# Delta rule of a two-model chain: gate rows in two buffers, strict matrices made two halves ahead, last merge on 64-wide blocks

## The chip, the cores and the metric

The kernel runs on 1 core of one Trainium2 chip. The metric is the device time of one execution in microseconds (us), 2837.27 us as the median of three runs. TensorE (PE), VectorE (DVE), ScalarE (ACT), GpSimd (POOL) and SyncE (SP) each work through a queue of their own in order; they meet only at semaphores. SP does nothing here but issue DMAs and wait.

## What is computed

The reference is a chain of layers on 528 tokens of width 1024, all in float32. The change touches one part of the first layer, the chunked gated delta rule over 16 value heads (`chunk_gated_delta_rule`):

```python
cum = jnp.cumsum(g, axis=-1)
decay = jnp.exp(jnp.where(causal, cum[..., :, None] - cum[..., None, :], -jnp.inf))
k_beta = k * beta[..., None]
a = jnp.where(strict, jnp.einsum('bhnid,bhnjd->bhnij', k_beta, k) * decay, 0.0)
sol = lax.linalg.triangular_solve(a + eye, rhs, left_side=True, lower=True, unit_diagonal=True)
u, w = sol[..., :dv], sol[..., dv:]
attn = jnp.einsum('bhnid,bhnjd->bhnij', q, k) * decay
def step(state, xs):
    v_new = u_c - jnp.einsum('bhck,bhkv->bhcv', w_c, state)
    o = jnp.einsum('bhck,bhkv->bhcv', q_c, state) + jnp.einsum('bhij,bhjv->bhiv', attn_c, v_new)
    state = state * last_c[..., None, None] + jnp.einsum('bhck,bhcv->bhkv', k_c, v_new)
```

Beside it the layer needs z, a projection of the same input (1024 to 2048 columns), whose blocks the kernel computes in the gaps of the delta rule.

## The kernel before

All of it is written out by hand, engine by engine, with semaphores; no planner chooses an order. The delta rule works on chunks of 106 tokens (`CH`), 5 of them, and on 8 of the 16 heads at a time: `HALVES` = 10 steps t, each two groups x of four heads. A step is called a half below. `pe_gdn`, `act_gdn`, `dve_gdn`, `pool_gdn` and `sp_gdn` hold one engine's part each, and in each a function `half(t)` or a loop over t.

A half needs the following, under the names of the profile.

- **Gate rows.** `g_D` (112 partitions x 8 heads x 106) is filled by a DMA that copies each head's cumulative gate to all partitions (`cum_rows`, L1214). `differences` subtracts the token's own gate (L1028) and adds a mask of large negative numbers (L1032), `decays` takes the exponential (L984), and `matrices` multiplies by beta (L1038) and by the product of keys that `kk` left in PSUM (L876, L1042). The result `g_AT` is the strict matrix of the half, in two buffers by t % 2. `decayed` makes `g_AN` = q k times decay (L1047) and is the last reader of `g_D`.
- **Small inverses.** `blocks_out` writes `g_AT` to HBM (L1222) and reads its 16x16 diagonal blocks back as `g_X`, one block to a partition (L1224). `small_inverses` (L1054 to L1086, blocks of 4, merged to 8) and `last_inverses` (to 16, then L1094 transposes) invert them on DVE. `blocks_back` (L1228, L1232) spreads them again as `g_blk`, and GpSimd's `expand` (L1173) makes block-diagonal matrices `g_U` and `g_TV` of them.
- **Merges.** Three times (`MERGES`, l = 0, 1, 2) the inverse grows by a level: TensorE transposes `g_U` (L927, not for l = 0), ACT copies that (L996), TensorE multiplies by `g_AT` (L938), ACT copies (L999), TensorE multiplies by `g_U` (L948), and DVE writes the new block under a mask (copy_predicated, L1135). All of it on the full 106x106.
- **State.** The value residual (L1107) reads the state `g_S`, which the half before wrote. After the merges TensorE applies the inverse (L955), DVE scales (L1141), TensorE makes the output and the state's increment (L965 to L969), GpSimd decays the state (L1188), DVE adds (L1145). Then L1047 makes `g_AN` of the next half.
- **z block.** In halves 0 to 5 TensorE also computes block z = t + 2 (`z_block`, 96 matmuls of L285 in two tiles), DVE evacuates each tile (`z_out`, L1101) into the one buffer `z_st`, and SP stores it (L1209). Its banks are those of the merges, so the merges wait for both. DVE splits weights for a later block at the half's end (L308), after which SP loads a new weight block (L2234). Halves 6 to 9 have no z block.

In half t, DVE's queue before is: keys (L1116), `differences(t+1)`, query decay (`g_EC`, L1123), `matrices(t+1)`, residual, both `z_out`, merge copy l = 0, `small_inverses(t+1)`, merge copy l = 1, `last_inverses(t+1)`, merge copy l = 2, L1141, then state and `g_AN` for each group, and the weight split. SP's queue, in half t, is `cum_rows(t+1)`, `blocks_out(t+1)`, two z stores, `blocks_back(t+1)`, `decay_rows(t+1)` (`g_EC`, L1217), the next weight load. `cum_rows(t+1)` waits until `g_AN` of half t is made, and `z_out` waits until the store before it has landed.

## Time and profile before

| | us |
|---|---|
| median of three runs | 2837.27 |
| lowest and highest | 2835.69, 2837.76 |
| profiled execution, its own time | 2833.87 |
| span of that execution | 2832.0 |
| ten halves of the delta rule in it | 309.6 to 714.7 |

The profile is one execution. Its page gives busy time of each engine, a chain of work that ended last, and groups of instructions by line. TensorE is busy for 91% of the whole span, but in 40 slices its digit falls to 7 or 8 in some of those that the delta rule covers, and the DMA engines move few bytes there. Times in the rows below count from the span's start.

### The profile page before, as it was taken

Reading aid. Unit: us, or ns where it says so; the run is one execution under the profiler, and the core shown is the slowest. Engines: PE = TensorE matmul, PEld = TensorE weight load, DVE = VectorE, ACT = ScalarE, POOL = GpSimd, SP = SyncE. Lnnn points to the kernel's source line nnn. Section 1 sums busy time; section 2 is a strip of 40 time slices with the busy share of each in tenths; the row PEclk is TensorE's granted clock in tenths of the full one; section 3 lists DMA queues with packets and bytes.
Section 4 is the critical chain, followed back from the end, with each engine's and each line's share of the span. In section 5 each row is a group of like instructions: output and inputs, shape, how many; then the busy total and the mean of one; then the engine's idle time right before and its main releaser. Section 6 shows DMA issues by size and latency. Waiting matters only on the chain.

```text
span 2832.0 us, 39867 instructions
## 1 busy us (share of the span) xinstructions
PE 2587.9 (91%) x16152; PEld 2269.9 (80%) x16152; DVE 1454.4 (51%) x2004; ACT 801.6 (28%) x1031; POOL 204.1 (7%) x166
## 2 busy tenths in 40 slices
PE   6998888868899999998998899999898778999998
PEld 6997888857799999998987688887685444688886
DVE  5776555655345344453364567667414555434433
ACT  5322222212422212231222322223222354323222
POOL 1000101011000000010000100002001200100001
PEclk9997999989699999999976999999898889899998
DMA  3222222231122222222200254444221000122221
GB/s 125 87 75 71 78 78 74 59 86 31 76 78 88 90 90 89 89 99 81 76 13 0 89 178 165 152 158 163 97 74 45 0 0 0 61 103 89 96 97 60
DMA packets 91921, 230.90 MB, mean 82 GB/s; under 512 B 59946, under 2 KB 61564, under 8 KB 67620
## 3 DMA queue, kind: packets, MB, share of 16 engines
q1 hardware_dynamic: 86272, 197.04, 21.6%
q10 hardware_dynamic: 5540, 32.30, 3.3%
q8 instruction: 82, 1.34, 0.2%
q14 instruction: 27, 0.22, 0.0%
HBM read 217.67 MB, written 11.64 MB: 81 GB/s over the span
## 4 chain that ended last, share of the span: by engine, by line
PE 78%; DVE 11%; DMA 4%; ACT 3%; issue 2%; POOL 0%; DVEq 0%; SPq 0%; ACTq 0%; POOLq 0%
PE ps L285 60%; DMA g_D<-scr_g 2%; PE ps L449 2%; PE ps L475 1%; PE ps L948 1%; PE ps L938 1%; PE ps L289 1%; DVE wlo L308 1%; PE ps L2122 1%; PE ps L2104 1%; DVE g_tmp L1082 1%; PE ps L1571 1%; PE ps L1572 1%; PE ps L955 1%; DVE a_mx L2188 1%
## 5 line engine op out<-in xcount | busy, mean ns | idle before, releaser
L285 PE MATMUL ps<-xa_hi,whi 128*128 128x264 f32 (+1 forms) x2512 | 656.4, 320 | 44.0 <-DVE wlo L308 19.8
L285 PE MATMUL ps<-xa_lo,whi 128*128 128x264 f32 (+1 forms) x2512 | 652.1, 319 | 0.0
L285 PE MATMUL ps<-xa_hi,wlo 128*128 128x264 f32 (+1 forms) x2512 | 649.8, 318 | 0.0
L308 DVE TENSOR_TENSOR wlo<-raw,whi 128x2048 fp32r<-128x2048 f32 x161 | 373.5, 2320 | 261.2 <-ACT whi L301 261.2
L285 PEld LDWEIGHTS ps<-xa_hi,whi 128*128 128x128 f32 x2512 | 419.2, 191 | 86.6 <-issue 33.2
L301 ACT ACTIVATE whi<-raw 128x2048 fp32r<-128x2048 f32 x161 | 307.5, 1910 | 598.0 <-PE ps L285 581.1
L285 PEld LDWEIGHTS ps<-xa_lo,whi 128*128 128x128 f32 x2512 | 419.4, 191 | 29.7
L285 PEld LDWEIGHTS ps<-xa_hi,wlo 128*128 128x128 f32 x2512 | 418.6, 191 | 30.3
L285 PE MATMUL ps<-xb_hi,whi 128*128 128x264 f32 (+1 forms) x1280 | 384.0, 340 | 9.9 <-DVE xb_lo L1688 8.1
L285 PE MATMUL ps<-xb_lo,whi 128*128 128x264 f32 (+1 forms) x1280 | 385.1, 341 | 0.0
L285 PE MATMUL ps<-xb_hi,wlo 128*128 128x264 f32 (+1 forms) x1280 | 383.6, 340 | 0.0
L285 PEld LDWEIGHTS ps<-xb_hi,whi 128*128 128x128 f32 x1280 | 220.5, 188 | 44.1 <-DVE xb_lo L1688 9.0
L285 PEld LDWEIGHTS ps<-xb_hi,wlo 128*128 128x128 f32 x1280 | 220.4, 189 | 27.5
L285 PEld LDWEIGHTS ps<-xb_lo,whi 128*128 128x128 f32 x1280 | 220.2, 189 | 27.6
L360 POOL TENSOR_TENSOR n_sq<-n_sq 128x512 f32<-128x512 f32 (+1 forms) x42 | 78.7, 1874 | 1403.1 <-ACT n_sq L370 1400.9
L643 DVE TENSOR_TENSOR h<-ps,h 128x528 f32<-128x528 f32 (+1 forms) x88 | 61.4, 698 | 189.1 <-PE ps L285 189.1
L580 ACT ACTIVATE xb_hi<-m_y 128x512 fp32r<-128x512 f32 (+1 forms) x96 | 61.1, 637 | 304.8 <-DVE m_y L620 280.7
L623 DVE TENSOR_TENSOR xb_lo<-m_y,xb_hi 128x512 fp32r<-128x512 f32 (+1 forms) x96 | 67.0, 698 | 67.5 <-ACT xb_hi L580 67.5
L645 DVE SCALAR_TENSOR_TENSOR h<-ps,b_mod,h 128x512 f32<-128x512 f32 x40 | 30.0, 751 | 123.2 <-PE ps L285 123.2
L938 PE MATMUL ps<-g_TV,g_AT 106*106 106x106 f32 x480 | 62.3, 293 | 30.4 <-DVE g_AT L1042 30.3
L938 PEld LDWEIGHTS ps<-g_TV,g_AT 106*106 106x106 f32 x480 | 58.6, 205 | 31.9 <-issue 30.8
L754 DVE SCALAR_TENSOR_TENSOR conv_acc<-conv_in,par,conv_acc 128x528 f32<-128x528 f32 x96 | 73.8, 769 | 11.3 <-DVE conv_acc L751 0.2
(386 smaller groups left out, 2919.8 us busy)
## 6 DMA issues: line engine op xcount, KB each, us to landing
raw<-weights SPq DMA_DIRECT2D x161, 1024.0 KB, 4.9
mod_w<-weights_mod ACTq DMA_DIRECT2D x24, 1024.0 KB, 4.8
g_EC<-scr_g SPq DMA_DIRECT2D x10, 424.0 KB, 4.8
scr_z<-z_st SPq DMA_DIRECT2D x16, 264.0 KB, 2.4
g_D<-scr_g SPq DMA_DIRECT2D x10, 371.0 KB, 6.2
scr_a<-g_AT SPq DMA_DIRECT2D x10, 318.0 KB
h<-x_in ACTq DMA_DIRECT2D x4, 528.0 KB, 8.2
z_a<-scr_z SPq DMA_DIRECT2D x1, 2112.0 KB, 12.4
```

What stands on the lines that cost most here:

```text
L285: mm = pe.matmul(ps[:, at_ + step * c + bank, 0:tn], w[:, hb.slot, k, c * P:(c + 1) * P], x[:, k, t0:t0 + tn], start=(k == 0 and n == 0), ...
L289: mm = pe.matmul(ps[:, 2 * c + 1, 0:en], w[:, hb.slot, k, c * P:(c + 1) * P], (elo if n == 1 else ehi)[:, k, 0:en], start=(k == 0 and n == ...
L301: act.activation(whi[:, hb.slot], raw[:, hb.raw_slot], ACT.Copy).then_inc(S("w_hi"), 1)
L308: dve.tensor_tensor(wlo[:, hb.slot], raw[:, hb.raw_slot], whi[:, hb.slot].bitcast(F32), ALU.subtract).then_inc(S("w_lo"), 1)
L360: pool.tensor_tensor(flat(sq[:, 0], pieces), flat(sq[:, 0], pieces), flat(sq[:, k], pieces), ALU.add)\
L449: mm = pe.matmul(ps[0:size, 4, bass.ds(i * (2 * heads) + (j * n * heads + first * heads), heads)], sq[:, buf, t:t + size], ones[:, 0:1] if ...
L580: act.activation(flat(xb_hi[:, t], pieces), flat(m_y[:, c], pieces), ACT.Copy).then_inc(S("two_hi"), 1)
L623: dve.tensor_tensor(flat(xb_lo[:, t], pieces), flat(m_y[:, c], pieces), flat(xb_hi[:, t], pieces).bitcast(F32), ALU.subtract).then_inc(S(" ...
L643: ins = dve.tensor_tensor(x, pair(c, pieces), x, ALU.add)
L645: ins = dve.scalar_tensor_tensor(x, pair(c, pieces), scale(2 * j + c), x, ALU.mult, ALU.add)
L754: ins = dve.scalar_tensor_tensor(conv_acc[:, c, :], x, w, conv_acc[:, c, :], ALU.mult, ALU.add)
L938: mm = pe.matmul(ps[0:CH, 4 * x, q * CH:(q + 1) * CH], g_AT[t % 2][0:CH, 4 * x + q, :], g_TV[0:CH, 4 * x + q, 0:CH], start=True, stop=True)
```

## The change

Memory: `g_D` becomes two buffers by t % 2, and `z_st` two by tile. The second of each lies in space behind `qkv`.

Gate rows: `differences` moves from DVE to GpSimd. `cum_rows(t+1)` is issued inside `blocks_out(t)`, and waits for `g_AN` of half t-1 instead of half t. So during half t the rows of half t+2 are fetched, `differences(t+2)` runs on GpSimd at the head of its half, `decays(t+2)` on ACT ahead of the last merge's copies, `kk(t+2)` on TensorE behind L955, into another bank, and `matrices(t+2)` on DVE behind L1141. The matrices of halves 0 and 1 are made ahead of the loop.

Inverses: `small_inverses(t+1)` now stands ahead of both `z_out`, and `last_inverses(t+1)` behind the first merge copy.

Last merge: for l = 2 the transposes, products and copies cover 64 or 42 columns instead of 106, and the masked copy becomes a plain one of 64 x 4 x 42.

```diff
+LOW = 4 * BLK
...
-z_st = at_r.take("z_st", [P, T])
...
-g_D, g_AT1 = (gw_r.take(f"g_{n}", [P, 8, CH]) for n in ("D", "AT1"))
+g_D0, g_AT1 = (gw_r.take(f"g_{n}", [P, 8, CH]) for n in ("D0", "AT1"))
+ge_r = Region(SB_G + 32 * TP * 4, SB_END)
+g_D1 = ge_r.take("g_D1", [P, 8, CH])
+z_st = (at_r.take("z_st0", [P, T]), ge_r.take("z_st1", [P, T]))
+g_D = (g_D0, g_D1)
...
 def pe_gdn(pe):
     def kk(t):
...
-            if t:
-                pe.wait_ge(S("g_kd"), nth(t - 1, x))
+            if t == 1:
+                pe.wait_ge(S("z_ev"), 2 * Z_EARLY + x + 1)
...
-                mm = pe.matmul(ps[0:CH, 4 * x, m * CH:(m + 1) * CH], k, k, start=True, stop=True)
+                mm = pe.matmul(ps[0:CH, 4 * x + (1 if t else 0), m * CH:(m + 1) * CH], k, k, start=True, stop=True)
...
     def qk(t):
...
-        if t < HALVES - 1:
-            kk(t + 1)
...
+        def freed(x):
+            pe.wait_ge(S("g_A"), nth(t + 1, x))
+            pe.wait_ge(S("g_an"), nth(t, x))
...
-            z_block(z, lambda x: pe.wait_ge(S("g_an"), nth(t, x)))
+            z_block(z, freed)
         for l in range(MERGES):
+            first, second = (slice(0, LOW), slice(LOW, CH)) if l == 2 else (slice(0, CH), slice(0, CH))
+            n, m = first.stop, second.stop - second.start
...
-                    if l == 1 and z < N_Z:
-                        pe.wait_ge(S("z_ev"), 2 + nth(z, x))
+                    if l == 1:
+                        if z < N_Z:
+                            pe.wait_ge(S("z_ev"), 2 + nth(z, x))
+                        elif t < HALVES - 1:
+                            pe.wait_ge(S("g_A"), nth(t + 1, x))
...
-                        mm = pe.transpose(ps[0:CH, 4 * x + 1, q * CH:(q + 1) * CH], g_U[0:CH, 4 * x + q, 0:CH], ident[0:CH, 0:CH])
+                        mm = pe.transpose(ps[first, 4 * x + 1, q * CH:q * CH + n], g_U[first, 4 * x + q, first], ident[first, first])
...
-                    if t < HALVES - 1:
-                        pe.wait_ge(S("g_A"), nth(t + 1, x))
...
-                    mm = pe.matmul(ps[0:CH, 4 * x, q * CH:(q + 1) * CH], g_AT[t % 2][0:CH, 4 * x + q, :], g_TV[0:CH, 4 * x + q, 0:CH],
+                    mm = pe.matmul(ps[second, 4 * x, q * CH:q * CH + n], g_AT[t % 2][first, 4 * x + q, second], g_TV[first, 4 * x + q, first],
...
-                    mm = pe.matmul(ps[0:CH, 4 * x + 2, q * CH:(q + 1) * CH], g_B1[0:CH, 4 * x + q, :], g_U[0:CH, 4 * x + q, 0:CH],
+                    mm = pe.matmul(ps[first, 4 * x + 2, q * CH:q * CH + m], g_B1[second, 4 * x + q, first], g_U[second, 4 * x + q, second],
...
+        if t < HALVES - 2:
+            kk(t + 2)
...
+    kk(1)
...
 def act_gdn(act):
     def decays(t):
...
-            act.wait_ge(S("g_part"), 6 * t + x + 3)
-            act.activation(heads4(g_D, x), heads4(g_D, x), ACT.Exp).then_inc(S("g_dec"), 1)
+            d = heads4(g_D[t % 2], x)
+            act.wait_ge(S("g_dif"), 4 * t + x + 3)
+            act.activation(d, d, ACT.Exp).then_inc(S("g_dec"), 1)
...
     def half(t):
...
-        if t < HALVES - 1:
-            decays(t + 1)
         for l in range(MERGES):
+            n = CH if l < 2 else LOW
+            if l == 2 and t < HALVES - 2:
+                decays(t + 2)
...
-                    act.activation(heads4(g_TV, x), four_of(4 * x + 1), ACT.Copy).then_inc(S("g_T"), 1)
+                    act.activation(heads4(g_TV, x, n, n), four_of(4 * x + 1, n)[:, :, 0:n], ACT.Copy).then_inc(S("g_T"), 1)
...
-                act.activation(heads4(g_B1, x), four_of(4 * x), ACT.Copy).then_inc(S("g_Pc"), 1)
+                rows = slice(0, CH) if l < 2 else slice(LOW, CH)
+                act.activation(g_B1[rows, 4 * x:4 * x + 4, 0:n],
+                               ps[rows, 4 * x, 0:4 * CH].rearrange("p (a t) -> p a t", a=4)[:, :, 0:n], ACT.Copy).then_inc(S("g_Pc"), 1)
...
-    for n in range(Z_EARLY):
-        act_split(act, HalfBlock(HB_GDN_OUT + n + 2))
+    act_split(act, HalfBlock(HB_GDN_OUT + 2))
+    decays(1)
+    act_split(act, HalfBlock(HB_GDN_OUT + 3))
...
     def per_pair(x, w=CH):
...
-    def differences(t):
-        dve.wait_ge(S("g_cum"), 16 * (t + 1))
-        for x, g in groups_of(t):
-            dve.tensor_tensor(heads4(g_D, x), heads4(g_D, x), tok(t, 0, g, CH), ALU.subtract).then_inc(S("g_part"), 1)
-        for x in range(2):
-            d = heads4(g_D, x)
-            dve.wait_ge(S("g_part"), 6 * t + x + 1)
-            dve.tensor_tensor(d, d, g_neg[0:CH, None, :].to_broadcast([CH, 4, CH]), ALU.add).then_inc(S("g_part"), 1)
...
     def matrices(t):
...
-            dve.tensor_tensor(heads4(a, x), heads4(g_D, x), tok(t, 32, g, CH), ALU.mult).then_inc(S("g_part"), 1)
+            dve.tensor_tensor(heads4(a, x), heads4(g_D[t % 2], x), tok(t, 32, g, CH), ALU.mult).then_inc(S("g_part"), 1)
...
-            dve.wait_ge(S("g_part"), 6 * t + x + 5)
-            dve.tensor_tensor(pairs(heads4(a, x)), per_pair(ps[0:CH, 4 * x, 0:2 * CH]), pairs(heads4(a, x)), ALU.mult)\
+            dve.wait_ge(S("g_part"), nth(t, x))
+            dve.tensor_tensor(pairs(heads4(a, x)), per_pair(ps[0:CH, 4 * x + (1 if t else 0), 0:2 * CH]), pairs(heads4(a, x)), ALU.mult)\
...
     def decayed(t, x):
...
-        dve.tensor_tensor(pairs(heads4(g_AN, x)), per_pair(ps[0:CH, 4 * x + 2, 0:2 * CH]), pairs(heads4(g_D, x)), ALU.mult)\
+        dve.tensor_tensor(pairs(heads4(g_AN, x)), per_pair(ps[0:CH, 4 * x + 2, 0:2 * CH]), pairs(heads4(g_D[t % 2], x)), ALU.mult)\
...
     def small_inverses(t):
...
     def z_out(n, c):
...
-        if 2 * n + c:
-            dve.wait_ge(S("z_out"), 16 * (2 * n + c))
-        dve.tensor_tensor(cols(z_st, FULL), ps[:, 1 + 4 * c:3 + 4 * c, 0:T // 2], cols(rstd, FULL), ALU.mult).then_inc(S("z_ev"), 1)
+        if n and c == 0:
+            dve.wait_ge(S("z_out"), 16 * 2 * n)
+        dve.tensor_tensor(cols(z_st[c], FULL), ps[:, 1 + 4 * c:3 + 4 * c, 0:T // 2], cols(rstd, FULL), ALU.mult).then_inc(S("z_ev"), 1)
...
     def residual(t, x, g):
...
-        if more:
-            differences(t + 1)
...
-        if more:
-            matrices(t + 1)
...
+        if more:
+            small_inverses(t + 1)
...
         for l in range(MERGES):
...
-                dve.copy_predicated(heads4(g_U, x), g_maskU[0:CH, l:l + 1, :].to_broadcast([CH, 4, CH]), four_of(4 * x + 2))\
-                    .then_inc(S("g_Uup"), 1)
-            if more and l < 2:
-                (small_inverses if l == 0 else last_inverses)(t + 1)
+                if l < 2:
+                    ins = dve.copy_predicated(heads4(g_U, x), g_maskU[0:CH, l:l + 1, :].to_broadcast([CH, 4, CH]), four_of(4 * x + 2))
+                else:
+                    ins = dve.tensor_copy(g_U[0:LOW, 4 * x:4 * x + 4, LOW:CH], four_of(4 * x + 2, LOW)[:, :, 0:CH - LOW])
+                ins.then_inc(S("g_Uup"), 1)
+            if more and l == 0:
+                last_inverses(t + 1)
...
+        if t < HALVES - 2:
+            matrices(t + 2)
...
-    differences(0)
...
+    matrices(1)
...
-    pool.wait_ge(S("g_set"), 16 * (N_BLK + 1))
+    def differences(t):
+        pool.wait_ge(S("g_cum"), 16 * (t + 1))
+        for x, g in groups_of(t):
+            d = heads4(g_D[t % 2], x)
+            own = g_tok[0:CH, t // 2, 4 * g:4 * g + 4][:, :, None].to_broadcast([CH, 4, CH])
+            pool.tensor_tensor(d, d, own, ALU.subtract).then_inc(S("g_dif"), 1)
+        for x in range(2):
+            d = heads4(g_D[t % 2], x)
+            pool.wait_ge(S("g_dif"), 4 * t + x + 1)
+            pool.tensor_tensor(d, d, g_neg[0:CH, None, :].to_broadcast([CH, 4, CH]), ALU.add).then_inc(S("g_dif"), 1)
...
+    pool.wait_ge(S("in"), IN_FIRST + 32)
+    differences(0)
+    differences(1)
...
+        if t < HALVES - 2:
+            differences(t + 2)
...
     def z_store(n, c):
...
-        sp.dma_start(scr_z[2 * n + c], z_st[:, :]).then_inc(S("z_out"), 16)
+        sp.dma_start(scr_z[2 * n + c], z_st[c][:, :]).then_inc(S("z_out"), 16)
...
     def cum_rows(t):
-        if t:
-            sp.wait_ge(S("g_an"), nth(t - 1, 1))
-        sp.dma_start(g_D[0:edge], scr_g[0, 8 * (t % 2):8 * (t % 2) + 8, chunk_cols(t)].partition_broadcast(edge)).then_inc(S("g_cum"), 16)
+        if t > 1:
+            sp.wait_ge(S("g_an"), nth(t - 2, 1))
+        sp.dma_start(g_D[t % 2][0:edge], scr_g[0, 8 * (t % 2):8 * (t % 2) + 8, chunk_cols(t)].partition_broadcast(edge)).then_inc(S("g_cum"), 16)
...
     def decay_rows(t):
...
     def blocks_out(t):
...
+        if t:
+            sp.wait_ge(S("g_exp"), 2 * t - 1)
...
+        if t < HALVES - 1:
+            cum_rows(t + 1)
...
-        sp.dma_start(scr_g[k], g_row[64 * k:64 * k + GH, :]).then_inc(S("g_rows"), 16)
+        sp.dma_start(scr_g[k], g_row[64 * k:64 * k + GH, :]).then_inc(S("g_set"), 16)
...
-    sp.wait_ge(S("g_rows"), 32)
+    sp.wait_ge(S("g_set"), 16 * (N_BLK + 3))
...
-    sp.wait_ge(S("g_set"), 16 * (N_BLK + 1))
...
-            cum_rows(t + 1)
```

DVE's queue, the rows of one half with a z block, from the weight split to the second merge copy. Before (numbers behind names are buffers; `g_AT_94` is one of the two `g_AT`):

```order
L308 TENSOR_TENSOR wlo<-raw,whi 128x2048
L1116 TENSOR_TENSOR g_KD<-ps,g_tok 106x512 x2
L1028 TENSOR_TENSOR g_D<-g_D,g_tok 106x424 x2
L1032 TENSOR_TENSOR g_D<-g_D,g_neg 106x424 x2
L1123 TENSOR_TENSOR g_EC<-qkv,g_EC 128x424 x2
L1038 TENSOR_TENSOR g_AT_94<-g_D,g_tok 106x424 x2
L1042 TENSOR_TENSOR g_AT_94<-ps,g_AT_94 106x424 x2
L1107 SCALAR_TENSOR_TENSOR g_VT<-ps,g_tok,g_VT 106x128 x8
L1101 TENSOR_TENSOR z_st<-ps,rstd 128x528 x2
L1135 COPY_PREDICATED g_U<-g_maskU,ps 106x4x106 x2
L1054 COPY g_X<-ones 56x16
```

The same place after:

```order
L1116 SCALAR_TENSOR_TENSOR g_VT<-ps,g_tok,g_VT 106x128 x8
L1063 COPY g_X<-ones 56x16
L1071 TENSOR_TENSOR g_tmp<-g_X 56x8
L1074 TENSOR_TENSOR g_X<-g_X,g_tmp 56x4x2
L1071 TENSOR_TENSOR g_tmp<-g_X 56x8
L1074 TENSOR_TENSOR g_X<-g_X,g_tmp 56x4x2
L1091 TENSOR_TENSOR g_tmp<-g_X 56x64 x2
L1095 TENSOR_REDUCE g_P_91<-g_tmp 56x16 x2
L1091 TENSOR_TENSOR g_tmp<-g_X,g_P_91 56x64 x2
L1095 TENSOR_REDUCE g_X<-g_tmp 56x4x4 x2
L1110 TENSOR_TENSOR z_st_103<-ps,rstd 128x528
L1110 TENSOR_TENSOR z_st_104<-ps,rstd 128x528
```

The four groups on `g_D` and `g_AT` are gone from the half's start, and the small inverses have moved in front of the evacuation of z.

SP's queue between the read of `g_EC` and the z stores of one half. Before:

```order
L1217 DMA g_EC<-scr_g 128x8x106
L2234 DMA raw<-weights 128x2048
L1214 DMA g_D<-scr_g 112x8x106
L1222 DMA scr_a<-g_AT_94 96x8x106
L1222 DMA scr_a<-g_AT_94 10x8x106
L1224 DMA g_X<-scr_a 56x16x16
```

After:

```order
L1244 DMA g_EC<-scr_g 128x8x106
L2263 DMA raw<-weights 128x2048
L1251 DMA scr_a<-g_AT_101 96x8x106
L1251 DMA scr_a<-g_AT_101 10x8x106
L1241 DMA g_D_100<-scr_g 112x8x106
L1255 DMA g_X<-scr_a 56x16x16
```

The two writes of `g_AT` now stand right behind the weight load, with the read of `g_D` (for a half later) behind them and ahead of the read of `g_X`.

## Rows read from the trace of the kernel before

**Rows 1.** Busy time by stretch: halves 0, 5, 6, 7 and 8; x is instructions.
```profile
core 0: us, PE busy (x) PEld busy (x) DVE busy (x) ACT busy (x) POOL busy (x), PEclk, DMA share, GB/s
309.60:352.10 42.50, 39.25 (x312) 37.58 (x311) 22.81 (x54) 10.22 (x17) 5.44 (x4) 0.90 0.27 68
...
531.90:574.60 42.70, 37.88 (x318) 36.06 (x317) 25.67 (x54) 10.20 (x18) 6.13 (x5) 0.96 0.28 72
574.60:615.00 40.40, 27.36 (x224) 25.58 (x222) 24.52 (x53) 8.52 (x17) 6.24 (x5) 0.83 0.28 63
615.00:656.70 41.70, 26.45 (x223) 24.68 (x222) 21.69 (x51) 8.47 (x17) 6.19 (x5) 0.84 0.35 88
656.70:691.00 34.30, 26.25 (x222) 24.49 (x221) 21.66 (x51) 8.44 (x16) 6.15 (x5) 0.90 0.24 44
```

**Rows 2.** Chain of waits in half 3: start us, us, what.
```profile
441.03 2.90 DVE wlo L308
...
444.75 6.32 DMA g_D<-scr_g
...
456.68 2.98 DMA scr_a<-g_AT
...
460.03 2.44 DMA scr_z<-z_st
462.57 0.72 DVE z_st L1101
```

**Rows 3.** Timeline of half 3, TensorE: state product, z block's first and last matmuls.
```profile
440.84 1.91 PE L912 MATMUL ps<-g_S,qkv 128*106 128x128 f32 x16
...
445.57 0.49 PE L285 MATMUL ps<-xa_hi,whi 128*128 128x264 f32 x2
...
457.13 0.41 PE L285 MATMUL ps<-xa_hi,wlo 128*128 128x264 f32 x2
```

**Rows 4.** DMA issues by line, 440 to 716 us: KB each, median us to landing.
```profile
raw<-weights SPq DMA_DIRECT2D x5, 1024.0 KB, 5.4
```

**Rows 5.** Timeline of half 3, DVE: first and last of the small inverses.
```profile
465.73 0.16 DVE L1054 COPY g_X<-ones 56x16 f32<-56x16 f32 x1
...
467.67 0.33 DVE L1086 TENSOR_REDUCE g_X<-g_tmp 56x16 f32<-56x64 f32 x2
```

**Rows 6.** Chain of waits in halves 5, 7 and 9: start us, us, what.
```profile
552.77 0.72 DVE z_st L1101
...
615.00 11.54 DMA g_D<-scr_g
...
636.69 0.65 DVE g_U L1135
...
641.21 0.64 DVE g_U L1135
...
645.70 0.55 DVE g_U L1135
...
694.33 2.07 DVE g_VT L1107 x8
...
701.57 0.65 DVE g_U L1135
...
706.13 1.97 PE ps L955 x16
```

**Rows 7.** Weight split (ns min/median/max) and the GpSimd instruction beside it in half 3.
```profile
L308 DVE TENSOR_TENSOR wlo<-raw,whi x7: 2293/2969/2978, 307.3 to 574.5; 128x2048 fp32r<-128x2048 f32 x7
...
439.69 2.09 POOL L1173 TENSOR_TENSOR g_TV<-g_blk,g_diag 106x896 f32<-106x896 f32 x1
```

**Rows 8.** GpSimd operations: count, busy us, mean ns, idle; L360 as ns min/median/max.
```profile
L1188 POOL TENSOR_TENSOR g_S<-g_S,g_lastB 128x512 f32<-128x512 f32 x20 | 21.0, 1050 | 28.6 <-PE ps L966 28.6
...
L360 POOL TENSOR_TENSOR n_sq<-n_sq x42: 1286/1610/2883, 12.7 to 2810.7; 128x512 f32<-128x512 f32 x24, 128x528 f32<-128x528 f32 x18
```

**Rows 9.** Timeline of half 8, keys' product; group of a plain PSUM copy on DVE.
```profile
658.22 0.91 PE L876 MATMUL ps<-qkv 128*106 128x106 f32 x8
...
L1996 DVE COPY r_cv<-ps 128x256 f32<-128x256 f32 x4 | 1.6, 408 | 0.0
```

## The prediction, made before the change was run

> **What bounds the kernel now.** I read first the busy time by stretch, cut at the ends of the ten halves. A half with a z block takes about 44.5 us (halves 1 to 5 fill 352.1 to 574.6), though TensorE has some 38 us in it; without one, halves 6 to 8 take 40.4, 41.7 and 34.3 us with 26 to 27 us of TensorE, and its granted clock falls to 0.83 and 0.84 [rows 1]. So the engine waits, and the question is for what. The chain of waits tells. Take half 3 and count τ from 441.0, the end of the last `g_AN`. The weight split runs to τ 2.9, the gate rows are then fetched until 10.1, DVE turns them into the strict matrix, which is written to HBM at 15.7, and behind that in SP's queue stands the first z store; `z_out` of the second tile waits for it and ends at 463.3, τ 22.3 [rows 2]. TensorE's timeline shows what this costs: the z block starts at 445.6 and is done at 457.5, 11.9 us, and then the merges wait [rows 3]. From the second `z_out` to the half's end is a chain of merges, state and output with little slack, 21.1 us in half 5, where TensorE's clock is 0.96 [rows 1, 6]. The bound is the latency of one half's preparation, which starts only when the half before has ended.
>
> **The change part by part.**
>
> *The gate rows leave the path.* Rows, differences, exponential and matrix of a half are now made a half earlier. What is late next? There are two candidates, and the second `z_out` must wait for both.
>
> First, the z block. It no longer waits for the keys' product behind the weight split, so it can start when L912 ends, 442.75, and end 11.9 us later, τ 13.7 [rows 3]. With one copy of 0.7, `z_out` could end at τ 14.4.
>
> Second, the small inverses, which now stand ahead of `z_out` in DVE's queue and need `g_X`. SP issues the weight load at τ 3.0, the writes of `g_AT` behind it, the read of `g_D` behind those, and `g_X` when the writes have landed. The weights land 5.4 us after their issue, τ 8.4 [rows 4]; `g_D`, next in the queue today, lands at τ 10.1, 1.7 later [rows 2]. The writes of `g_AT` have nearly its size and take its place, so they land at 10.1 at the latest, and `g_D` about 11.8. `g_X` is issued near 10 and has `g_D` in front of it; it lands between 11.8 and 13.2 (a whole 3.0 us as the writes take [rows 2]). I take the middle, 12.5. The small inverses take 2.3 us [rows 5].
>
> *GpSimd beside DVE.* The four differences on GpSimd cost more than on DVE: two with one broadcast input, as L1188, 1.05 x 424/512 = 0.87 us each, and two with a mask, as the fastest L360, 1.29 x 424/512 = 1.07 us [rows 8], together 3.9 us. They need `g_D`, so they run from τ 11.8 to 15.7, beside the small inverses. That the two engines disturb each other stands in the trace: the weight split takes 2.3 us at its fastest and 2.97 in the median, and in half 3 GpSimd's L1173 covers its first 0.84 us [rows 7]. So the price for the small inverses lies between nothing and the 3.2 us of GpSimd work left at 12.5. Some of their instructions are reduces of short products that may run beside it, so I take 2.0. They end at τ 12.5 + 2.3 + 2.0 = 16.8, later than the z block, and both `z_out` (1.4) end at 18.2, where 22.3 and 21.6 (half 5, 553.5) stand now [rows 2, 6].
>
> The Trainium skill (SBUF — State Buffer, "Who interferes with whom") says that a DVE instruction with two SBUF inputs and a GpSimd instruction that reads SBUF exclude each other for the whole of the first one. The trace agrees: 0.7 lost of 0.84 covered [rows 7]. By that rule the sum would take nearly 3.2 instead of 2.0 in seven halves; that is the second rival.
>
> *Merges.* `last_inverses` moves from the third merge to the second. In half 7 it takes 3.85 us (641.85 to 645.70), while the first merge's copy ends 4.5 before the second's [rows 6]. Now the second ends 3.85 + 1.3 (two copies) = 5.2 later: +0.7. The third took 4.4 us behind the inverses (641.85 to 646.25); without them half 9 shows 3.9 (702.22 to 706.13) [rows 6]. With 64 columns for 106 at most 40% of that goes, 1.6 us, at least nothing. The masked copies take 0.64 us and a plain one of 256 columns takes 0.41 [rows 6, 9], so I take 1.2: the third merge takes 2.7, a gain of 1.7. `kk(t+2)` now stands on TensorE's path behind L955, 0.91 us [rows 9], part of which fits a wait for DVE's L1141: +0.6, bounds 0.3 and 0.9. Its `matrices` on DVE (four of 0.6) lie in DVE's wait for GpSimd's state decay, and `decays` on ACT in the wait for the second merge; if GpSimd were over 5 us late that cover would go and ACT's copies with it. Net -0.4: from `z_out` to the end 21.1 becomes 20.7, and from the first merge copy in half 7 (637.3 to 656.7, 19.4) it becomes 19.0, or 18.4 without `kk`.
>
> *Prologue.* The later wait for set-up DMAs delays one weight load by about 2 us that is needed some 30 us later, and the differences of halves 0 and 1 on GpSimd lie beside z blocks: nothing.
>
> *Sum.* With z block: 18.2 + 20.7 = 38.9 us.
> - Halves 1 to 5: 5 x (44.5 - 38.9) = 28.0.
> - Half 0 is counted from the end of its split, 2.9 later: 42.5 - 36.0 = 6.5.
> - Half 6: a weight load but no z block, 16.8 + 1.3 + 19.0 = 37.1 against 40.4: 3.3.
> - Half 7: today `g_D` waits behind the load of all z and lands at 626.5, 11.5 after the half's start [rows 6]; with the writes in front it lands at 13.2 and `g_X` at 13.9. So 13.9 + 4.3 + 1.3 + 19.0 = 38.5 against 41.7: 3.2.
> - Half 8: no differences. `g_EC` is the last to come, as in half 9, where the residual ends at 696.4, 5.4 after its start [rows 6]. 5.4 + 2.3 + 1.3 + 18.4 = 27.4 against 34.3: 6.9.
> - Half 9: 1.2 from the narrow merge.
>
> Together 49.1 us. The profiled execution, 2833.9, becomes 2784.8; the median of the runs lies 3.4 above it, so 2788.2, in round 2788.
>
> **The rivals.**
>
> *The ports cost nothing.* If GpSimd runs between DVE's short instructions, seven halves are 2.0 shorter: 14 us, 2774. For it: the small inverses' instructions are 0.2 to 0.4 us long and wait for each other [rows 5]. Against: the split's 2.97 [rows 7].
>
> *Full exclusion.* The small inverses wait for all that GpSimd has left, 3.2 instead of 2.0 in seven halves: +8.4, 2797. For it: the split lost nearly all that was covered. (This is the rule of the Trainium skill cited above.)
>
> *The narrow merge gives nothing.* If its fixed costs dominate, each of ten halves is 1.2 longer: +12, 2800. The Trainium skill (TensorEngine Tiling (Array Packing), "Key Properties") says that a change of tiling mode drains the array; no row here shows such a change.
>
> *Slower: z held behind a late `g_X`.* The small inverses stand ahead of `z_out`, and both merges and the state wait for `z_out`. If weight load, writes and two reads in one queue slow each other down, every half with this queue pays. The gain of 49 in seven halves is 7.0 each, so it is used up when `g_X` lands at τ 19.5 instead of 12.5; at 21 the loss is 7 x 1.5 = 10.5, 2848. For it: `g_D` took 11.5 us once behind 2 MB [rows 6]. Against: that was a transfer of twice the size, and behind the weights it takes 6.3 [rows 2].
>
> **How the numbers follow.** Forecast 44%, no port cost 20%, full exclusion 18%, narrow merge without gain 10%, slower 4%, something within 0.2% of no change, from causes that I don't see, 4%. The likeliest time is 2788. Around it: `g_X` at 11.8 or 13.2 is 5 us either way, the merge's bounds 4 down and 12 up, `kk` 3 either way. Downwards the range takes in the first rival with `g_X` early, 2774 - 5 - 3 = 2766; upwards the second and third and a late `g_X`, to 2808. A measurement of this kernel can tell about 0.2%, 5.7 us, from no change. Faster by more: 92%; within: 4%; slower: 4%.
>
> **What would show it.** The chain of a half with z should have no `g_D` in it: weight split, weight load or write of `g_AT`, small inverses, `z_out`, merges. `g_X` should be there at τ 12.5 and the second `z_out` end at 18.2; halves 1 to 5 take 38.9 us each, and half 8 some 27.4 with `g_EC` in the chain. The products of the small inverses (L1071, L1091) should be longer than now where GpSimd's L1194 and L1198 run, those of the last inverses not. The third merge should take 2.7 us. TensorE's clock in these stretches should rise. The prediction is wrong if the z block, or ACT behind late differences, ends the wait instead, or if `g_X` comes behind τ 15.

## The result, and the profile after

The changed kernel takes 2811.08 us (median of five runs, 2804.76 to 2817.53) against 2835.69 (2834.50 to 2837.76) before: a ratio of 0.9916, 95% interval 0.9902 to 0.9931. It is faster, by 24.6 us, half of the 49 that the forecast of 2788 gave; the time lies above the range of 2766 to 2808. The profiled execution took 2809.6 us, with a span of 2807.7.

Busy time by stretch, cut at the ends of the halves as in [rows 1]; here halves 0, 2, 3, 5, 6, 8 and 9 (half 7 takes 37.9):

```profile
core 0: us, PE busy (x) PEld busy (x) DVE busy (x) ACT busy (x) POOL busy (x), PEclk, DMA share, GB/s
311.00:348.50 37.50, 36.46 (x312) 34.97 (x312) 23.85 (x49) 9.60 (x17) 9.29 (x8) 0.93 0.33 77
...
389.90:428.40 38.50, 35.65 (x319) 34.30 (x318) 26.36 (x50) 9.59 (x17) 9.91 (x9) 0.96 0.34 81
428.40:469.10 40.70, 37.05 (x318) 35.75 (x317) 26.98 (x50) 9.59 (x17) 9.93 (x9) 0.92 0.32 76
...
509.40:553.00 43.60, 39.07 (x319) 37.67 (x318) 27.14 (x50) 9.59 (x17) 9.91 (x9) 0.88 0.31 71
553.00:590.80 37.80, 24.98 (x222) 23.51 (x221) 24.78 (x48) 7.68 (x16) 9.83 (x9) 0.82 0.33 67
...
628.70:661.20 32.50, 27.83 (x214) 26.32 (x213) 16.91 (x43) 6.79 (x14) 6.16 (x5) 0.79 0.20 34
661.20:686.70 25.50, 22.75 (x192) 21.31 (x190) 10.04 (x22) 5.70 (x12) 2.77 (x3) 0.87 0.06 9
```

Read the second number (duration) with PEclk. Half 2, at clock 0.96, takes 38.5 us, close to the 38.9 of the forecast. Half 5 has the same instructions, clock 0.88 and 43.6 us. The halves with a z block now last 41.4, 38.5, 40.7, 40.3 and 43.6 us (halves 1 to 5), and the slower ones have the lower clock. Half 5 before had 0.96 [rows 1]. All ten halves together went from 405.1 to 375.7 us.

The chain of waits in half 3 (start us, us, what), to be read beside [rows 2]. The half starts at 428.4, so τ is the time less that:

```profile
428.30 2.92 DVE wlo L312
...
432.09 6.97 DMA scr_a<-g_AT
439.08 2.05 DMA g_X<-scr_a
...
446.49 3.18 PE ps L958 x16
...
451.35 2.30 PE ps L948 x16
...
455.30 0.65 DVE g_U L1143
...
458.63 1.94 PE ps L965 x16
```

DVE's timeline has both `z_out` in one row:

```profile
445.65 1.31 DVE L1110 TENSOR_TENSOR z_st<-ps,rstd 128x528 f32<-128x528 f32 x2
```

`g_D` is gone from the chain, and `g_X` is there at τ 12.7. The first `z_out` ends at τ 18.0 and lets TensorE go on with L958, the second ends at τ 18.6. Then L958 takes 3.18 us for its 16 products and L948 2.30, where 1.6 is the time of either at full clock. TensorE's timeline of half 5 (start us, us, line, operation, idle time before in brackets) shows both places where that happens:

```profile
527.95 3.13 PE L958 MATMUL ps<-g_U,g_B 106*106 106x106 f32 x16 [3.69 <-DVE z_st L1110]
...
538.19 1.92 PE L958 MATMUL ps<-g_U,g_B 42*64 42x42 f32 x16
540.04 3.75 PE L965 MATMUL ps<-g_VT,g_U 106*106 106x128 f32 x16
543.58 1.63 PE L880 MATMUL ps<-qkv 128*106 128x106 f32 x8
```

The first stands behind an idle stretch of 3.69 us, in which TensorE waits for `z_out`. The second stands right behind the narrow merge. The same 16 products of L965 (L955 before) took 1.97 us [rows 6]. In both places the granted clock falls to 0.50, that is 1.2 GHz in place of 2.4. The second place shows in L965's durations over the stage (ns min/median/max), in this kernel and in the one before:

```profile
L965 PE MATMUL ps<-g_VT,g_U x160: 272/417/547, 336.4 to 678.6; 106*106 106x128 f32 x160
```

```profile
L955 PE MATMUL ps<-g_VT,g_U x160: 272/273/329, 341.8 to 707.8; 106*106 106x128 f32 x160
```

GpSimd and DVE work beside each other in half 3. First GpSimd's timeline, then DVE's:

```profile
440.51 1.74 POOL L1194 TENSOR_TENSOR g_D<-g_D,g_tok 106x424 f32<-106x424 f32 x2 [11.46 <-DMA g_D<-scr_g]
442.22 1.96 POOL L1198 TENSOR_TENSOR g_D<-g_D,g_neg 106x424 f32<-106x424 f32 x2
```

```profile
441.47 0.80 DVE L1071 TENSOR_TENSOR g_tmp<-g_X 56x8 f32<-56x8 f32 x1
442.31 0.93 DVE L1074 TENSOR_TENSOR g_X<-g_X,g_tmp 56x8 f32<-56x8 f32 x1
443.28 0.92 DVE L1071 TENSOR_TENSOR g_tmp<-g_X 56x8 f32<-56x8 f32 x1
444.24 0.16 DVE L1074 TENSOR_TENSOR g_X<-g_X,g_tmp 56x8 f32<-56x8 f32 x1
```

A DVE product of eight columns takes 0.16 us alone and 0.80 to 0.93 while GpSimd works: each ends when the GpSimd instruction under way has ended. The small inverses take 4.5 us, 2.2 more than the 2.3 of [rows 5].

Half 8, in the chain, in DVE's timeline and in TensorE's:

```profile
632.57 2.13 DMA g_X<-scr_a
...
636.92 1.14 DVE L1143 COPY_PREDICATED g_U<-g_maskU,ps 106x424 f32<-106x424 uint32 x2
```

```profile
637.60 1.66 PE L939 MATMUL ps<-ident,g_U 106*106 106x106 f32 x8 [4.21 <-DVE g_U L1143]
639.16 3.21 PE L948 MATMUL ps<-g_TV,g_AT 106*106 106x106 f32 x16
...
648.46 3.75 PE L965 MATMUL ps<-g_VT,g_U 106*106 106x128 f32 x16
```

The two copies of the first merge end at τ 9.4 where 9.0 was forecast, though by `g_X` and not by `g_EC`. From there to the half's end it takes 23.1 us in place of 18.4, with L948 behind a wait of 4.2 us and L965 behind the narrow merge at the lower clock.

### The profile page after: what moved, and what is told of

Its sections match the earlier page's. It is cut to its first block, busy times and chain, and to the rows that moved or that the text cites. A ratio compares the mean times of both kernels' runs of the same rounds, so it can differ in the third digit from the quotient of the medians.

```text
span 2807.7 us, 39879 instructions
## 1 busy us (share of the span) xinstructions
PE 2582.4 (92%) x16152; PEld 2266.7 (81%) x16152; DVE 1457.9 (52%) x1964; ACT 794.9 (28%) x1031; POOL 241.2 (9%) x206
## 4 chain that ended last, share of the span: by engine, by line
PE 79%; DVE 11%; DMA 4%; ACT 3%; issue 2%; SPq 0%; DVEq 0%; POOL 0%; ACTq 0%; POOLq 0%
PE ps L289 60%; DMA scr_a<-g_AT 2%; PE ps L453 2%; PE ps L479 1%; PE ps L958 1%; DVE wlo L312 1%; PE ps L965 1%; PE ps L293 1%; PE ps L2151 1%; PE ps L948 1%; PE ps L2133 1%; PE ps L1600 1%; PE ps L1601 1%; DMA g_X<-scr_a 1%; DVE a_mx L2217 1%
## 5 line engine op out<-in xcount | busy, mean ns | idle before, releaser
L289 PEld LDWEIGHTS ps<-xa_lo,whi 128*128 128x128 f32 x2512 | 418.8, 191 | 29.5
L289 PEld LDWEIGHTS ps<-xb_lo,whi 128*128 128x128 f32 x1280 | 221.1, 189 | 27.4
L621 DVE SCALAR_TENSOR_TENSOR m_act<-ps,rstd 128x528 f32<-128x528 f32 (+1 forms) x64 | 44.6, 696 | 50.1 <-PE ps L289 48.4
L958 PE MATMUL ps<-g_U,g_B 106*106 106x106 f32 (+1 forms) x480 | 54.1, 275 | 15.6 <-DVE z_st L1110 15.5
```

Of the source, the lines that this page charges most:

```text
L289: mm = pe.matmul(ps[:, at_ + step * c + bank, 0:tn], w[:, hb.slot, k, c * P:(c + 1) * P], x[:, k, t0:t0 + tn], start=(k == 0 and n == 0), ...
L621: dve.scalar_tensor_tensor(cols(m_act[:, c], pieces), pair(c, pieces), 0.0, cols(rstd, pieces), ALU.max, ALU.mult)\
L958: mm = pe.matmul(ps[first, 4 * x + 2, q * CH:q * CH + m], g_B1[second, 4 * x + q, first], g_U[second, 4 * x + q, second], start=True, stop ...
```

## The experiments

Two theories stood against each other for what was missing. By the first (theory I in the expectations), TensorE's clock of 1.2 GHz behind its wait for `z_out` takes it, the idle stretch. By the second (theory N), the narrow merge itself brings that clock. Beside them stood GpSimd's port, and SP's queue with `g_X` behind a weight load. Every kernel was timed in four to ten runs, and the ratio is to the kernel before. The half durations are of one profiled execution each. The kernel before, run again beside each group of kernels, has medians from 2831.8 to 2836.5 us, so a difference between kernels of different groups is uncertain by some 4 us. "Time at the lower clock" adds up how long the clock stood at 0.50 within the ten halves, from stretches of 0.5 us and good to about 2 us: about 71 us before and 89 after.

### e1_wide_merge: the change without its narrow merge

```diff
-  first, second = (slice(0, LOW), slice(LOW, CH)) if l == 2 else (slice(0, CH), slice(0, CH))
+  first, second = (slice(0, LOW), slice(LOW, CH)) if l > 2 else (slice(0, CH), slice(0, CH))
```

ScalarE's and DVE's copies are set back to full width with it.

> The changed kernel with the last merge on the full 106x106 again. In the changed kernel TensorE's granted clock is 0.5 for some 3.3 us right behind the narrow merge in six of ten halves (L965 takes 3.2 to 3.7 us for 16 instructions there, 1.9 to 2.0 elsewhere). Theory N, the narrow merge brings the low clock: L965 takes 2.0 us in all halves, half 9 takes 23.7 us instead of 25.6, and the total is about the same, 2808 to 2814, since ten halves lose 1.2 to 1.7 us each and six get back some 2.5. Theory I, only idle time ahead of the first merge brings it: L965 stays at 3.6 us in some halves, half 9 at 25.6, and the total rises by 12 to 15 us, to about 2825.

Measured: 2808.19 us, ratio 0.9917 (0.9903 to 0.9930). L965's 16 products are short in every half, 273 ns in the median:

```profile
L965 PE MATMUL ps<-g_VT,g_U x160: 272/273/329, 339.1 to 682.7; 106*106 106x128 f32 x160
```

The last half takes 23.6 us as before the change, in place of 25.5, and the time at the lower clock falls from 89 to 69 us. Yet the total cannot be told from that of the change: what the narrow products save they lose again behind the merge. The idle stretch ahead of L958 is still there, 2.5 to 3.6 us, and halves 1 to 5 take 42.0, 39.2, 42.1, 41.2 and 41.6. In half 2, with a wait of 2.46 us, the clock stays at 1.00.

### e2_narrow_alone: the narrow merge in the kernel before

The other way round: the kernel before with the last merge's transposes, products and copies on 64-wide blocks, and nothing else.

> The kernel before with the narrow last merge alone. Theory N: L955 behind it takes 3.6 us in some halves, half 9 takes 25.6 us instead of 23.7, and the total is within 5 us of 2835.7. Theory I: L955 stays at 2.0 us, half 9 gets 1.2 us shorter, 22.5, and since the last inverses still stand behind the second merge copy the other halves gain less: total 2830.

Measured: 2854.46 us, ratio 1.0086 (1.0058 to 1.0114). The narrow merge, a change that takes work away, costs some 22 us by itself. That was not expected: theory N had the total within 5 us of the kernel before, theory I below it. What theory N said of the clock is there. The products of L958 (L955 in the kernel before) have a median of 421 ns, and the time at the lower clock is 130 us against 71:

```profile
L958 PE MATMUL ps<-g_VT,g_U x160: 272/421/547, 337.3 to 724.2; 106*106 106x128 f32 x160
...
383.87 3.72 PE L958 MATMUL ps<-g_VT,g_U 106*106 106x128 f32 x16 [1.37 <-DVE g_U L1144]
```

In this kernel the narrow merge has next to nothing to give in halves 0 to 8. The last inverses still stand on DVE between the second merge's copy and the third's, and take 3.9 us; from the one copy to L958 it is 4.2 us, and 4.5 before. TensorE gets done earlier and waits longer ahead of L958, in the nine halves (TensorE's idle time, us and times, here and then in the kernel before):

```profile
  DVE g_U L1144: 13.5, 9
...
  DVE g_U L1135: 6.4, 9
```

So the narrow merge's loss here goes with a longer wait behind it, 1.5 us in place of 0.7, and e2 alone can't part the two.

### e11_narrow_padded: the same with the gaps filled

Is it the shape of the products, or that TensorE has little to do for some microseconds? Into e2_narrow_alone go full-width products that nobody reads, behind the narrow merge's transposes and behind its first products:

```diff
+  if l == 2:
+      for _ in range(3):
+          pe.matmul(ps[:, 3, 0:P], ident[:, :], ones[:, :], start=True, stop=True)
```

> e2_narrow_alone (the kernel before with only the last merge in 64-wide blocks, 2854.5 us against 2831.8 us for the kernel before) with three more full-width products behind the merge's transposes and three behind its first products, in the engine's waits for ScalarE and VectorE; nothing reads their results. Theory A (the narrow merge lowers the clock because TensorE has little work for some us in it): the time at 1.2 GHz in the stage falls from 130 us to 60 to 80 us, L965's 16 products take about 2.0 us, total 2828 to 2838. Theory S (the shape of the narrow products itself brings it): the low stretches behind the merge stay, total 2848 to 2860.

Measured: 2835.47 us, ratio 1.0007 (0.9995 to 1.0019), 19 us faster than without the added work. The same 160 products:

```profile
L966 PE MATMUL ps<-g_VT,g_U x160: 272/273/329, 339.5 to 708.0; 106*106 106x128 f32 x160
```

The time at the lower clock is 67 us. So in this kernel the shape does no harm by itself; that TensorE has little work around the narrow products does. The added products cost next to nothing on the path, as the last inverses on DVE fill that time: from the second merge's copy to L966 it is 4.3 us, with 4.2 in e2. For the same reason there is hardly a gain to have over the kernel before.

### e3_late_differences: GpSimd off the small inverses

```diff
+  pool.wait_ge(S("g_sb"), X_STEPS * (t + 1) + 13)
```

The wait stands on GpSimd ahead of the gate differences, until DVE has done the small inverses.

> The changed kernel with GpSimd's differences held until the small inverses of the half are done (a wait on g_sb), so that the two no longer run beside each other. Theory P, the shared port: in seven halves three or four of L1071 and L1074 take 0.8 to 0.95 us instead of 0.16, the small inverses 4.4 instead of 2.3. They return to 2.3, TensorE idles 2.1 us less ahead of the first merge, and the total falls by 15 us or more, to 2796 or below. Rival: the wait for g_X sets the pace and DVE has slack: the small inverses get shorter, the total stays at 2811. A third outcome is that the exponentials on ACT, now behind later differences, hold the last merge: then ACT's L998 has a wait on POOL ahead of it and the total rises.

Measured: 2798.08 us, ratio 0.9870 (0.9854 to 0.9886), 13 us faster than the change (9 by the distance of each from the kernel before in its own group), a little less than the 15 expected. DVE's timeline of half 3, from a first product of the small inverses to `z_out`:

```profile
437.75 0.16 DVE L1071 TENSOR_TENSOR g_tmp<-g_X 56x8 f32<-56x8 f32 x1
...
439.78 1.30 DVE L1110 TENSOR_TENSOR z_st<-ps,rstd 128x528 f32<-128x528 f32 x2
```

They take 2.24 us (437.54 to 439.78) in place of 4.5, which settles the port's price at 2.2 to 2.3 us a half. A part of it comes back: GpSimd now works from 439.9 to 443.6, and the first product of the last inverses takes 1.61 us in place of 1.01. The halves with z keep two lengths, 38.2 and 38.4 at clock 0.96, 39.9 to 40.0 at 0.91. TensorE's wait for `z_out` in half 3 is down to 0.86 us and L958 behind it runs at full clock, yet L965 behind the narrow merge takes 3.75, with no wait above 1.22 us in between.

### e4_filler and e5_wide_late_filler: work in the idle stretch

Twelve products per group of heads (24 in all) that nobody reads, between the first merge's first and second products, where TensorE otherwise idles; e4_filler is the change with that, e5_wide_late_filler adds the edits of e1 and e3.

```diff
+  if l == 0 and t < HALVES - 1:
+      for _ in range(12):
+          pe.matmul(ps[:, 3, 0:P], ident[:, :], ones[:, :], start=True, stop=True)
```

> The changed kernel with 12 extra products (ident by ones, 128 columns, into a bank that nothing reads) on TensorE between the first merge's first and second product, in halves 0 to 8; the results are not used. They fill most of the 3.2 us in which TensorE idles there, at 444 to 446.5 us in half 3, before its clock falls to 0.5 for 6.5 us. Theory I: with the gap filled the clock stays high, L958 of l = 0 takes 1.7 us instead of 2.6 to 3.2, the second merge 1 us less, total 2795 to 2800. Rival, the clock falls for other reasons: no change in L958, and the total rises by up to 1 us a half where the fillers outlast the wait, to 2815.

Measured: 2791.0 us, ratio 0.9860 (0.9844 to 0.9875), 20 us faster than the change (16 by the distances from the kernel before), and better than the 2795 to 2800 expected. TensorE's timeline of half 3:

```profile
444.26 2.86 PE L954 MATMUL ps<-ones,ident 128*128 128x128 f32 x24
446.96 1.66 PE L962 MATMUL ps<-g_U,g_B 106*106 106x106 f32 x16
...
456.91 1.97 PE L969 MATMUL ps<-g_VT,g_U 106*106 106x128 f32 x16
```

The first merge's second products take 1.66 us in place of 3.18, and L969 behind the narrow merge 1.97 as well. Halves 1 to 4 take 38.1, 37.9, 37.8 and 37.8 us at clock 1.00: with the idle stretch filled the low clock is gone at both places. It is not gone for good: in half 5 (40.4, clock 0.96) L969 takes 3.56 behind the narrow merge. Half 0 lost (41.9, clock 0.88).

> The changed kernel with the last merge on full width, GpSimd's differences behind the small inverses, and the 12 extra products ahead of the first merge's second product (their results are not used). Theory S, the miss of the prediction is TensorE's clock and the shared port: with both out of the way a half with z block takes 16.4 us to the end of the second z_out and 21.1 from there, 37.5; the ten halves take about 352 us where the changed kernel's take 375.7, and the total is 2786. If something else holds the halves, the ten stay above 365 us and the total above 2798. The fillers may outlast the now shorter wait, up to 1.5 us in a half.

Measured: 2798.36 us, ratio 0.9874 (0.9858 to 0.9891), not the 2786 expected. Halves 1 to 5 are alike, 39.2 or 39.3 us, at clock 1.00. But the added products last 2.86 us and end 1.4 us after the second `z_out` (447.0 for 445.65 in half 3), so they stand on the path themselves, and at full clock the full-width merge costs its own time. A filler longer than the wait gives back a part of what it brings.

### e8_before_filler: the same filler in the kernel before

> The kernel before with the same 12 extra products ahead of the first merge's second product (results not used). Its TensorE idles 3.3 us there in half 3 and then runs at the low clock. If a filled gap keeps the clock, L948 of the first merge and L938 of the second get faster in the four or five halves that are at the low clock there, 1.5 to 2 us each: total 2823 to 2827. If it doesn't, the total stays at 2832 or rises.

Measured: 2833.75 us, ratio 1.0001 (0.9991 to 1.0010): no gain, where 2823 to 2827 was expected. Halves 1 to 5 go from 44.5 to 43.7 us on average, but halves 6, 7 and 8 lose 1.7, 2.6 and 3.6. There the kernel before waits so long that the clock is down when the filler comes, and it then takes 3.61 us on the path:

```profile
623.24 3.18 PE L938 MATMUL ps<-g_TV,g_AT 106*106 106x106 f32 x16 [13.71 <-DVE g_AT L1046]
626.22 3.61 PE L944 MATMUL ps<-ones,ident 128*128 128x128 f32 x24
```

### e7_one_z_buffer: the change with a single z tile

```diff
-  z_st = (at_r.take("z_st0", [P, T]), ge_r.take("z_st1", [P, T]))
+  z_st = (at_r.take("z_st0", [P, T]),) * 2
```

> The changed kernel with one z_st buffer as before, the rest of the change kept. The second z_out again waits for the first store, 2.4 us and its issue: six halves get 2.1 to 2.5 us longer and TensorE idles longer, total 2824 to 2830. If the second buffer is worth nothing, because the wait for g_X would cover the store, the total stays at 2811; this can't be, as the first z_out itself stands behind g_X.

Measured: 2812.2 us, ratio 0.9919 (0.9903 to 0.9936), the time of the change itself where 2824 to 2830 was expected. The chain of half 3 does have the store between the two copies:

```profile
449.86 2.04 DMA scr_z<-z_st
...
452.00 0.72 DVE z_st L1110
```

The second copy ends at τ 20.8 in place of 18.6. The first is not later (17.9 for 18.0), so half of L958's products start as before, and halves 1 to 5 grow by 1.8 us only (42.7 on average against 40.9). The ten halves together are 7.6 us longer, and the execution makes up 2.6 of it behind them, where nothing was changed, and 1.9 ahead; the medians do not resolve the rest. What the second tile is worth stays open, below some 8 us.

### e6_early_writes: `g_AT` and `g_X` ahead of the weight load

e1 and e3 together, and SP issues the writes of `g_AT` and the reads of `g_X` two halves ahead, at the end of a half and before the next weight load:

```diff
-                if t < HALVES - 1:
-                    blocks_out(t + 1)
...
+                    if t < HALVES - 2:
+                        writes(t + 2)
...
+                    if t < HALVES - 2:
+                        read_back(t + 2)
+                    if t < HALVES - 3:
+                        cum_rows(t + 3)
```

> The changed kernel with the last merge on full width, the differences behind the small inverses, and, in SP's queue, the writes of g_AT and the read of g_X for half t + 2 issued at the end of half t, ahead of the weight load, instead of behind it in half t + 1. No fillers. Theory X, the wait for g_X behind the weight load is what ends last ahead of z_out: then the small inverses run at 7.4 to 9.7 us in a half, z_out waits for TensorE alone and ends at 14.5, TensorE never idles there and keeps its clock: 36 us for a half with z block; halves 6 and 7 take some 31.5, half 8 29, half 9 23.6; sum about 331, total about 2765. Rival Q, the queue only moves the wait: the read of g_EC lands later and holds the residual, and the halves stay at 39 us.

Measured: 2768.74 us, ratio 0.9772 (0.9755 to 0.9788), 42 us faster than the change and 29 faster than e3, from which it differs by the queue's order and by the full-width merge. The chain of half 3:

```profile
423.28 11.75 PE ps L289 x96
435.03 1.49 PE ps L948 x16
```

No DMA is left in it, and no idle stretch: z block and merges follow each other at clock 1.00, and halves 1 to 5 take 36.7 us each. In halves 6 to 8 nothing fills the wait for `g_EC`, and the lower clock is still there:

```profile
571.12 1.66 PE L939 MATMUL ps<-ident,g_U 106*106 106x106 f32 x8 [3.98 <-DVE g_U L1143]
572.68 3.21 PE L948 MATMUL ps<-g_TV,g_AT 106*106 106x106 f32 x16
```

### e9_early_narrow: e6 with the narrow merge

> The changed kernel with the three edits of e6_early_writes (GpSimd's gate differences late, the writes and reads of g_AT and g_X for the half after next issued at the end of a half ahead of the weight load) but with the last merge in 64-wide products again, so against e6_early_writes one edit: the last merge's width. In e6_early_writes the z halves last 36.7 us with TensorE at clock 1.00 and without idle stretches, the stage takes 337.2 us. Theory D (narrow products cost clock only together with TensorE's idle stretch ahead of them): L965's 16 products stay near 2.0 us, the merge's gain of about 1.2 us a half comes through, z halves 35 to 35.8 us at clock 0.98 or more, total 2755 to 2762. Theory N (the narrow merge brings the low clock by itself): L965's 16 products take 3.2 to 3.7 us in most halves, the z halves stay at 36.5 us or longer, total 2767 to 2775.

Measured: 2762.11 us, ratio 0.9743 (0.9727 to 0.9759), the fastest kernel of the study. Against e3 it differs by the order in SP's queue alone, so that order is worth 36 us (38 by the distances from the kernel before). On the clock neither theory has it all. Halves 2 and 5 take 35.2 us at clock 1.00, 1.5 less than with full width; halves 1, 3 and 4 take 36.8, 38.5 and 38.4 at 0.95 and 0.91. TensorE's timeline in half 3 (the half's z block starts at 420.3):

```profile
442.54 1.22 PE L958 MATMUL ps<-g_U,g_B 42*64 42x42 f32 x16
443.71 3.74 PE L965 MATMUL ps<-g_VT,g_U 106*106 106x128 f32 x16
```

No wait here is longer than 0.61 us, and the clock falls all the same: the narrow merge can bring it down without an idle stretch, in some halves and not in others.

### e10_early_filler and e12_all: fillers in the late halves, and everything together

e10_early_filler is e6 with ten products per group ahead of the second merge's transposes from half 6 on.

> e6_early_writes with 10 more 128-row products, whose results nothing reads, on TensorE in halves 6 to 9 ahead of the second merge's transposes, where the engine otherwise idles about 4 us behind the load of g_EC. Theory C (the idle stretch is what brings the clock of 1.2 GHz in the steps behind it): L948's products of l = 1 take 1.7 us instead of 3.2 us, halves 6 to 8 last 28.5 to 29.5 us instead of 30.3 to 30.7, total 2762 to 2765. Rival (the added products stand on the path and the low clock comes from an earlier stretch): halves 6 to 8 unchanged or longer, total 2768 to 2773.

Measured: 2766.79 us, ratio 0.9766 (0.9749 to 0.9782). The time at the lower clock falls from 28 to 13 us, half 8 from 30.5 to 28.9 (clock 1.00), the whole of the ten halves by 1.5. Halves 6 and 7 take 31.1 and 30.1 us after 30.7 and 30.3, not the 28.5 to 29.5 expected. The medians, 2.0 apart, can hardly tell that.

> e9_early_narrow (2762.1 us, stage 334.2 us) with the two fillings that e10_early_filler and e11_narrow_padded showed apart: 10 products nobody reads ahead of the second merge in halves 6 to 9, and 3 and 3 in the narrow merge's waits. Theory A (TensorE's little work brings the lower clock): the 16 products of L965 take about 2.0 us in every half, the z halves last 35.0 to 35.6 us, each at clock 0.98 or more, halves 6 to 8 below 29.5 us, total 2752 to 2758. Rival (the added products cost on the path what the clock gives): z halves 36 us or more, total 2760 to 2764.

Measured: 2771.54 us, ratio 0.9776 (0.9762 to 0.9789): slower than e9, of which it is the padded version, and slower than either theory had it. In halves 1 to 5 the padding does keep the clock at 1.00, but they take 36.8 or 36.9 us, 1.6 more than e9's undisturbed 35.2. In halves 6 and 7 the clock is down for 10.2 and 13.7 us, in each from the start of the narrow merge on (548.8 and 582.8), behind a wait of 1.1 us:

```profile
582.63 1.15 PE L943 MATMUL ps<-ident,g_U 64*64 64x64 f32 x8 [1.14 <-DVE g_U L1155]
...
590.58 3.75 PE L977 MATMUL ps<-g_VT,g_U 106*106 106x128 f32 x16
```

So the padding of e11 does not keep the clock everywhere. e10, with the same fillers ahead of the second merge but a full-width third one, has 3.4 us of it in each of these halves. Why it falls here and not in halves 1 to 5, these runs don't say.

## Why the gain was half of what was predicted

**Up to the second `z_out` every step held within half a microsecond.** In half 3 `g_X` landed at τ 12.7 (12.5 predicted), the small inverses took 4.5 us (4.3), and the second `z_out` ended at τ 18.6 (18.2), against 22.3 before; over halves 1 to 5 it is 18.5 in the mean, 0.3 late. The port's price was 2.2, where 2.0 was taken between bounds of 0 and 3.2. The Trainium skill (SBUF — State Buffer, "Who interferes with whom") was right on the mechanism: each of DVE's two-input products ends with the GpSimd instruction that it meets, 0.80 to 0.93 us for 0.16. It lost less than all of GpSimd's time, since the copy ahead of them (0.28) and one product at each boundary got through. The rival of no port cost is refuted by e3; that of full exclusion priced the loss 1.0 too high.

**The third merge held.** 2.7 us (455.94 to 458.63) were predicted and measured in half 3. At full clock the narrow width is worth 1.5 (e6 against halves 2 and 5 of e9), where 1.2 was taken. A drain between the tiling modes, on which the fourth case leaned, is not to be seen in that time.

**The step that failed is the term for the rest of the half: "from `z_out` to the end 21.1 becomes 20.7", and with it the terms 18.4 in half 8 and 1.2 in half 9.** It has two errors, and both are TensorE's clock.

The first error is where the 21.1 comes from: half 5, because the half shown there had clock 0.96 [rows 1]. From the second `z_out` to the half's end, halves 1 to 5 of the kernel before take 23.6, 22.5, 23.0, 24.0 and 21.1 us, 22.9 in the mean. TensorE's timeline in the kernel before, in half 3 and in half 5, shows why half 5 is the exception:

```profile
463.42 1.74 PE L948 MATMUL ps<-g_U,g_B 106*106 106x106 f32 x8 [3.34 <-DVE z_st L1101]
...
466.64 2.51 PE L938 MATMUL ps<-g_TV,g_AT 106*106 106x106 f32 x16
...
553.63 0.96 PE L948 MATMUL ps<-g_U,g_B 106*106 106x106 f32 x8 [1.38 <-DVE z_st L1101]
...
555.73 1.77 PE L938 MATMUL ps<-g_TV,g_AT 106*106 106x106 f32 x16
```

Behind an idle stretch of 1.38 us the products run at full clock. Behind the 2.6 to 3.3 of halves 1 to 4 the clock falls, in halves 1 and 3 at once, in halves 2 and 4 a microsecond or two later; L938 takes 2.5 to 3.1 us in all four. The sum took the mean half of before, 44.5, off against the tail of the fastest one, which is worth 5 x 1.75 = 8.8 of the 10.0 us missing in halves 1 to 5. The change kept the stretch (2.5 to 3.7 us), so "TensorE's clock in these stretches should rise" was wrong too. The later second `z_out`, 18.5 for 18.2, is another 1.6; the edits themselves give 0.4 back.

The second error is what the narrow merge brings. In halves 1 to 5 it does not show in the sum: the edits' own net of -0.4 came out at -0.5 (the same tails after are 22.4, 20.6, 22.0, 22.4 and 24.4, in the mean 22.4), but by luck: two wrong parts cancel. Against e1, the change with full width, the narrow merge gave 0.4 a half there and not 1.2. In halves 1, 4 and 5 the steps behind it lost to the clock what it saved: in half 5 the narrow L958, L965 and L880 take 0.75, 1.8 and 0.7 longer than in half 3. The rest of the edits cost nothing (22.7 in e1 after 22.9) where +0.8 was taken. Over all ten halves e1 takes 378.0 us and the change 375.7, so the narrow merge gave 2.3 us of the 12 that the sum has for it. e2 shows that it can cost: there the mean tail goes from 22.9 to 24.7.

In half 8 the 18.4 was derived from half 7 of the kernel before, from its first merge copy on. In that half the low clock stood ahead of this copy, in the first merge behind a wait of 14.0 us for `g_AT`, and all that follows ran at full clock. After the change the first merge is done early and the wait, 4.2 us, stands ahead of the second, so the low clock falls into the tail: from the second merge's first product to the third's it is 7.1 us, with 5.2 taken, in e1 as well (7.0). That is 1.9 of the 5.1 missing, and the later start is 0.4. The narrow merge is 2.8: it was to give 1.2 and cost 1.6 (e1 has 30.9 us in this half). In half 9 it was to give 1.2 and cost 1.8.

**Where the 25 us are**, by the profiled executions (predicted gain 49.1, measured 24.3). Half 0: 37.5 instead of 36.0, 1.5. Halves 1 to 5: 204.5 instead of 194.5, 10.0. Halves 6 and 7: 75.7 instead of 75.6, 0.1. Half 8: 32.5 instead of 27.4, 5.1. Half 9: 25.5 instead of 22.5, 3.0. The prologue lost 1.4, put down at nothing: the ten halves start at 309.1 to 311.7 us in the kernels with the change and at 306.5 to 309.6 in those without, so the change seems to cost some 3 us there. Behind the ten halves the execution took 3.7 longer; over all kernels of the study that part varies from 2114.2 to 2121.0, and e1, with the same instructions there, has 2116.2, so an effect of the change is not shown. Together 24.8.

**The rivals.** The case "the narrow merge gives nothing", 2800, came true in its effect and nearly in its size (9.7 of its 12 us in the ten halves), with another mechanism: it isn't a fixed cost of the products but the clock of what comes behind them. The slower case, a late `g_X`, didn't come: `g_X` was at τ 12.7, not 19.5. But the same queue was the largest reserve: e9, with the writes and reads ahead of the weight load, is 36 us below e3, and nothing else differs.

The Trainium skill (TensorE: Matmul & The Clock Gate, "HAM oscillation — how this bites in real kernels") says that waits for data between stretches of matmuls let TensorE's clock drop, and that the work behind them then starts at the half rate. The traces agree: 3.18 us for 1.6 behind an idle 3.2 us, and 1.66 with the wait filled (e4), though not in every case, as half 2 of e1 keeps the clock behind 2.46 us. Taken seriously, it would have kept the tail at 22.9 - 0.4 as long as the wait stays: 5 x 1.75 us more, 2797, inside the range. What is above that is mostly halves 8 and 9, the prologue and the scatter behind the ten halves.
